# Output projection of all token tiles but the last, done inside the attention stage of a two-layer diffusion backbone

## The chip, the cores and the metric
One Trainium2 chip, one of its eight cores. The metric is the device time of one execution of the whole kernel in microseconds (us), as the median of several executions. Before the change three executions took 1636.07, 1642.16 and 1647.30 us, so the median is 1642.16 us.

## The reference
The kernel computes a two-layer backbone over 256 latent tokens and 256 context tokens of width 1024, all in fp32. Each layer is a mixer followed by a mixture of experts; the parts that matter here are these (layer 0 mixes with latent attention and a linear recurrence, layer 1 with windowed attention and a state-space model):

```python
# mixer, either layer: heads of attention beside a recurrence, then one output projection
y_l = jnp.concatenate([attn_l, other_l], axis=-1) @ w_out      # w_out: 1024 x 1024
# the layer adds it to the stream through a gate row, normalises, and routes to experts
x = x + gate * y
h = rmsnorm(x, norm2_g) * (1 + scale) + shift
x = x + gate2 * moe_ffn(h, router_w, router_b, w_gate, w_up, w_down)
# moe_ffn: 32 experts of 3 x 1024 x 512 weights, each token goes to its best two
```

Layer 0 does this for latent and context tokens, layer 1 for latent tokens alone.

## The kernel before
The tokens lie in tiles of 128: tiles 0 and 1 are latent, 2 and 3 context. Layer 0 works on four tiles, layer 1 on two. The kernel is a series of stages. Each stage is a block in which every engine has its own program in order, engines meet only by semaphores, and nothing of the next block starts before the block ends. For one layer the stages that matter are `attention_stage`, `output_front_stage`, `experts_stage` and a combine stage.

**Attention** (L856 to L1029). The work is a list of units, one head of one tile, tile by tile: 32 units in layer 0, 16 in layer 1, taken in pairs (16 and 8 pairs; four pairs finish a tile). In turn `j` of TensorE's loop (L934) it computes the scores of pair `j+1` (`score`), turns the probabilities of the two units of pair `j` through the identity (`turn`), and multiplies those of pair `j-1` with the values (`values`). ScalarE copies turned probabilities out and takes exponentials. VectorE finds the maxima, divides the probabilities by their sum (L1017, L1018), which is what `turn` waits for, and then copies the finished pair `j-1` out of bank 6 (`copy_out`, L1004). Units of the latent tiles see 4 blocks of keys, those of the context tiles 2. In layer 0 six products of the late modulation rows (`md`) are put after `values` of turns 3, 5, 7, 9, 11 and 13, in bank 7 (L943 to L949); VectorE takes each one out a turn later. SyncE loads their weights and `w_out` here (L882, L2255); in layer 1 it loads `w_out` and the first expert weights, a third of slot 2 and a spare one (L2293 to L2298).

**Output and router** (`output_front_stage`, L1103 to L1380). TensorE multiplies each tile's 1024 mixed features by `w_out` in half tiles of 512 columns (`project`, L1184), rotating over four banks. A half tile is 8 matmuls of 128x128 by 128x512; the profile shows an fp32 matmul as two instructions. VectorE multiplies the bank by the gate row and adds it to the token stream (`add`, L1257 and L1258), ScalarE squares the finished tile and takes the root (`root`, L1155), VectorE scales it (`scale`, L1261), and TensorE turns it (L1193). After the last tile the router's products follow, the choice of experts on VectorE, and the ranks. Before its first `add`, VectorE waits for the router's small tables (L1274).

**SyncE's order in that stage** (L1128 to L1146) is gate rows, modulation columns, router tables, then `first_weights`: rows of the norm, and in layer 0 the whole of expert 0 and the down matrix of expert 1. Slot 1 of the expert weights is where `w_out` lies, so its gate and up matrices wait for all projections (L1136); those of slot 2 wait for the last `add` (L1138), the rest for `h_ready` and `part_logits`. In layer 0 GpSimd writes 4 MB of zeros to spare blocks meanwhile.

**Experts** (`experts_stage`, L1428). There are three slots (`RING`), so three experts and a spare down matrix can be there before the stage begins. From then on SyncE loads the next expert into a slot when the gate and up product of its last block is done (L1462). An expert is 6 MB.

The lines that set the order around the change:

```python
            for j in range(pairs):                     # TensorE, attention, L934
                ...score of pair j+1; turn(2 * j); turn(2 * j + 1)
                if j:
                    values(j - 1)
                if j in ada_after: ...md.product(a, 7)
```

Of the kernel before, what the change touches and what calls it, by code (L numbers as in the profile page):

```python
# [20 lines left out]
ALU = mybir.AluOpType  # L21
# [3 lines left out]
P = 128  # L25
D = 1024
KC = D // P
SEQ = 256
NT = 4
# [826 lines left out]
def attention_stage(c, units, qt, kt, v_of, scale, dst_t, p, pt, width, sink=None, mask=None, sp_work=None, md=None):  # L856
# [11 lines left out]
    if md:  # L868
        ada_after = {3 + a * (pairs - 6) // (md.n - 1): a for a in range(md.n)}
        ada_in = [c.sem(f"ada_w_in{j}") for j in range(len(md.ring))]  # L870
        ada_product, ada_done, stored, preset, tables_in, columns = (
            c.sem(x) for x in ("ada_product", "ada_row_done", "mod_stored", "mod_tables_preset", "mod_tables_in", "cond_columns"))
    nm, rs, es = ([c.stat[:, a + s:a + s + 1] for s in range(4)] for a in (0, 4, 8))

# [3 lines left out]
    with nc.Block() as block:  # L878
        @block.sync
        def _(sp):  # L880
            if md:
                for a in range(len(md.ring)):  # L882
                    if a == 1:
                        sp.wait_ge(tables_in, 16 * md.n_loads)
                    md.load_weights(sp, a, ada_in[a])
            if sp_work:
                sp_work(sp)
            if md:
                R = len(md.ring)
                for a in range(R, md.n):  # L890
                    sp.wait_ge(ada_product, a - R + 1)
                    md.load_weights(sp, a, ada_in[a % R])
                sp.wait_ge(ada_done, md.n)
                md.store(sp, stored)
                sp.wait_ge(stored, 16 * md.Q * len(md.segments))
# [9 lines left out]
        def _(pe):  # L905
# [28 lines left out]
            for j in range(pairs):  # L934
                for u in (2 * j + 2, 2 * j + 3):
                    if u < n:
                        score(u)
                turn(2 * j)
                turn(2 * j + 1)
                if j:  # L940
                    values(j - 1)
                if j in ada_after:
                    a = ada_after[j]  # L943
                    if a == 0:
                        pe.wait_ge(columns, 1)
                    else:
                        pe.wait_ge(ada_done, a)
                    pe.wait_ge(ada_in[a % len(md.ring)], 16 * (a // len(md.ring) + 1))
                    md.product(a, 7).then_inc(ada_product, 1)  # L949
            values(pairs - 1)  # L950
# [26 lines left out]
        def _(dve):  # L977
# [32 lines left out]
            for u in range(n):  # L1010
                k0 = units[u][2]
                dve.wait_ge(exp_r, u + 1)
                den = rs[u % 4]
                if sink is not None:
                    dve.wait_ge(den_r, u + 1)
                    step(nc.vector.tensor_tensor(den, den, es[u % 4], ALU.add))
                step(nc.vector.reciprocal(den, den))  # L1017
                nc.vector.tensor_scalar(p[:, u % 4, k0 * P:T], p[:, u % 4, k0 * P:T], den, None, ALU.mult).then_inc(p_ready, 1)  # L1018
                if u + 2 < n:
                    maximum(u + 2)  # L1020
                j = u // 2
                if u % 2 and j:
                    copy_out(j - 1)
                    if j - 1 in ada_after:
                        if ada_after[j - 1] == 0:
                            dve.wait_ge(tables_in, 16 * md.n_loads)
                        dve.wait_ge(ada_product, ada_after[j - 1] + 1)
                        md.finish(ada_after[j - 1], 7, ada_done)
# [4 lines left out]
YB = 4  # L1033

# [68 lines left out]
def output_front_stage(c, m, tiles, wo, halves, gates_at, tmp_at, sp_work, pool_work=None, pool_done=None):  # L1103
# [5 lines left out]
    gate_in, product, taken = S("out_gate_in"), S("out_product"), S("out_added")  # L1109
# [9 lines left out]
    gates = [c.scr[:, gates_at + s * D:gates_at + (s + 1) * D] for s in streams]  # L1119
    tmp = c.scr[:, tmp_at:tmp_at + BANK]  # L1120
    units = [(t, q) for t in tiles for q in range(2)]
# [4 lines left out]
    with nc.Block() as block:  # L1126
        @block.sync
        def _(sp):  # L1128
            for s in streams:
                sp.dma_start(gates[s], mod_row(c, s, m.layer, 2)).then_inc(gate_in, 16)  # L1130
# [5 lines left out]
            sp.wait_ge(product, len(units))  # L1136
            load_gate_up(c, m, sp, 1, 1)
            sp.wait_ge(taken, len(units))  # L1138
# [15 lines left out]
        def _(act):  # L1154
            def root(t):  # L1155
                act.wait_ge(taken, 2 * t + 2)
# [26 lines left out]
        def _(pe):  # L1183
            def project(u):  # L1184
                t, q = units[u]
                if u >= 4:
                    pe.wait_ge(taken, u - 3)
                for k in range(KC):
                    src = halves[k // 4][:, k % 4, t * P:(t + 1) * P]
                    last = nc.tensor.matmul(c.ps[u % 4][:], src, wo[:, k, q * BANK:(q + 1) * BANK], start=k == 0, stop=k == KC - 1)  # L1190
                last.then_inc(product, 1)

# [11 lines left out]
            def part_product(s):  # L1204
# [5 lines left out]
                pe.wait_ge(taken, len(units) if s else 2 * nt - 3)  # L1210
# [7 lines left out]
            for t in tiles:  # L1218
                project(2 * t)
                project(2 * t + 1)  # L1220
                if t:
                    turn(t - 1)
# [3 lines left out]
            turn(nt - 1)  # L1226
# [23 lines left out]
        def _(dve):  # L1250
            step, go, wait, v = c.dve_chain.step, c.dve_chain.go, c.dve_chain.wait, nc.vector

            def add(u):
                t, q = units[u]
                dve.wait_ge(product, u + 1)
                cols = slice(q * BANK, (q + 1) * BANK)
                step(v.tensor_tensor(tmp, c.ps[u % 4][:], gates[t // LT][:, cols], ALU.mult))  # L1257
                step(v.tensor_tensor(c.x[:, t, cols], c.x[:, t, cols], tmp, ALU.add))  # L1258
                dve.sem_inc(taken, 1)
# [28 lines left out]
            dve.wait_ge(gate_in, 16 * len(streams))  # L1288
            for t in tiles:
                add(2 * t)  # L1290
                if t:
                    scale(t - 1)
                if t == NT - 1:
                    dve.wait_ge(m.rows_in, 16 * len(streams))
                    rows(0)
                    rows(1)
                add(2 * t + 1)
            scale(nt - 1)
# [927 lines left out]
def program(nc, ins, outs):  # L2226
    with ExitStack() as ctx:
# [29 lines left out]
        def clear_spare_blocks(pool):  # L2257
# [4 lines left out]
            for r in parts:  # L2262
# [3 lines left out]

        units = [(h, t, 0 if t < LT else LT) for t in everyone for h in range(NH)]
        attention_stage(c, units, m.qt, lambda h: m.kt[:, h, :], lambda h, k: m.v[:, k, h * VD:(h + 1) * VD],
                        QK ** -0.5, m.attn_t, m.p, m.pt, QK, sp_work=loads, md=last)
# [9 lines left out]
        output_front_stage(c, mo, everyone, m.wo, (m.attn_t, m.gr), 9216, 3072, first_weights, clear_spare_blocks, blocks_cleared)  # L2279
# [13 lines left out]
        def loads(sp):  # L2293
# [5 lines left out]

        units = [(h, t, 0) for t in range(LT) for h in range(NH)]  # L2300
        attention_stage(c, units, m.qt, lambda h: m.kt[:, h // (NH // KVH), :],
                        lambda h, k: m.kv[:, k, KVH * HD + h // (NH // KVH) * HD:KVH * HD + (h // (NH // KVH) + 1) * HD],
                        HD ** -0.5, m.attn_t, m.p, m.pt, HD, sink=m.sink, mask=lambda t: (1 - t, m.far[:, t, :]), sp_work=loads)
# [4 lines left out]
        output_front_stage(c, mo, range(LT), m.wo, (m.attn_t, m.y_t), 9216, 8192, first_weights)  # L2308
# [49 lines left out]
```

## Time and profile before

| | us |
|---|---|
| median of three executions | 1642.16 |
| lowest, highest | 1636.07, 1647.30 |
| the profiled execution | 1640.26 |
| its span on the core | 1638.4 |
| TensorE matmul busy | 1231.4 (75%) |
| TensorE weight load busy (beside matmul) | 716.8 (44%) |
| VectorE busy | 540.6 (33%) |
| ScalarE busy | 404.5 (25%) |
| bytes moved | 515.12 MB, mean 314 GB/s |

All durations in this document come from that one profiled execution, whose 1640.26 us are its span of 1638.4 us and 1.9 us around it. The busy shares are averages over stages with different limits; what bounds a stage is read from that stretch alone. PE is TensorE, PEld its weight load, DVE VectorE, ACT ScalarE, POOL GpSimd, SP SyncE (SPq its queue). "<-" in brackets names what ended the idle time ahead of an instruction.

### The profile page before, as it was taken

The page shows a single profiled execution, that of the slowest core. Times are in us where ns is not written, and L with a number is a line of the kernel's source. Part 1 is how long each engine was busy: PE and PEld are TensorE (multiplying, and loading weights), DVE is VectorE, ACT ScalarE, POOL GpSimd, SP SyncE. Part 2 cuts the span into 40 slices and gives each one's busy share as a digit, 9 for nine tenths or more (in the row PEclk, how much of TensorE's full clock was granted, in tenths as well). Part 3 has the DMA queues.
Part 4 walks back from the last instruction along what each step waited for, and adds up shares of the span by engine and source line. Part 5 has one row for each costly group of instructions (what it writes and reads, how often), then busy time and mean ns, then how long its engine had stood idle before and what let it go on. Part 6 is the DMA issues. An engine that isn't in the chain of part 4 may idle for free. (4 is left out here: it accounts for less than half of the span.)

```text
span 1638.4 us, 34883 instructions
## 1 busy us (share of the span) xinstructions
PE 1231.4 (75%) x14230; PEld 716.8 (44%) x14231; DVE 540.6 (33%) x1490; ACT 404.5 (25%) x927; POOL 39.3 (2%) x83
## 2 busy tenths in 40 slices
PE   4897887897799997777662898888579766655652
PEld 3354654543465554444331646544345433322321
DVE  1537564526322222111113456873511111101102
ACT  1253233412132222212202222641122221111110
POOL 0001101010000000000001000000000000000000
PEclk8899898998899998989886899979699887777776
DMA  8311896485899999999996410083799999999995
GB/s 312 121 67 39 305 379 248 171 318 247 342 416 429 429 428 430 428 429 429 429 428 251 170 52 0 1 359 105 332 419 428 429 429 429 429 428 428 429 428 208
DMA packets 84160, 515.12 MB, mean 314 GB/s; under 512 B 13917, under 2 KB 18242, under 8 KB 58746
## 3 DMA queue, kind: packets, MB, share of 16 engines
q1 hardware_dynamic: 74664, 489.60, 72.8%
q10 hardware_dynamic: 5730, 13.81, 2.2%
q0 software_dynamic: 3696, 10.73, 1.7%
q8 instruction: 50, 0.82, 0.2%
q14 instruction: 20, 0.16, 0.0%
HBM read 497.10 MB, written 17.01 MB: 314 GB/s over the span
## 5 line engine op out<-in xcount | busy, mean ns | idle before, releaser
L1509 PE MATMUL bank<-sb_ring,sb_scratch 128*32 128x256 f32 x3904 | 272.8, 441 | 150.4 <-DMA sb_ring<-in_moe_w_up 138.9
L1509 PEld LDWEIGHTS bank<-sb_ring,sb_scratch 128*32 128x32 f32 x3904 | 144.7, 127 | 276.1 <-issue 220.9
L1590 DVE TENSOR_TENSOR sb_scratch<-sb_scratch,bank 128x128 f32<-128x128 f32 x88 | 25.3, 288 | 700.3 <-ACT sb_scratch L1543 700.3
L1547 ACT ACTIVATE sb_scratch<-bank 32x256 f32<-32x256 f32 x352 | 131.8, 374 | 273.8 <-PE bank L1519 270.7
L1509 PE MATMUL bank<-sb_scratch 128*32 128x256 f32 x1728 | 118.7, 436 | 60.8 <-DMA sb_scratch<-in_moe_w_up 56.6
L1489 PE MATMUL bank<-sb_h,sb_scratch 128*32 128x256 f32 x2256 | 141.1, 384 | 6.1 <-DVE sb_scratch L1577 6.1
L1543 ACT ACTIVATE sb_scratch<-bank 128x128 f32<-128x128 f32 x88 | 24.4, 277 | 423.8 <-PE bank L1509 423.7
L1519 PE MATMUL bank<-sb_ring,sb_scratch 128*32 128x256 f32 x1856 | 111.5, 380 | 8.5 <-issue 8.2
L1509 PEld LDWEIGHTS bank<-sb_scratch 128*32 128x32 f32 x1728 | 62.2, 125 | 116.0 <-issue 91.8
L1489 PEld LDWEIGHTS bank<-sb_h,sb_scratch 128*32 128x32 f32 x2256 | 74.8, 111 | 54.8 <-DVE sb_scratch L1577 6.6
L1519 PEld LDWEIGHTS bank<-sb_ring,sb_scratch 128*32 128x32 f32 x1856 | 62.7, 110 | 51.2 <-issue 19.8
L1190 PE MATMUL bank<-sb_ring,sb_scratch 128*128 128x512 f32 x160 | 69.9, 593 | 0.6 <-PEq L878 0.6
L1921 PE MATMUL bank<-sb_ht,sb_ring 128*128 128x512 f32 (+1 forms) x192 | 64.9, 496 | 0.0
L551 PE MATMUL bank<-sb_ht,sb_ring 128*128 128x512 f32 x128 | 58.3, 618 | 6.8 <-PEq L253 6.8
L1519 PE MATMUL bank<-sb_scratch 128*32 128x256 f32 x864 | 51.9, 380 | 4.5 <-issue 4.1
L1582 DVE STREAM_TRANSPOSE sb_scratch<-bank 128x256 f32<-128x256 f32 x90 | 38.9, 432 | 37.4 <-PE bank L1489 37.4
L194 PE MATMUL bank<-sb_ring 128*32 128x128 f32 x1344 | 44.4, 291 | 8.6 <-DMA sb_ring<-in_ada_w 8.6
L1921 PEld LDWEIGHTS bank<-sb_ht,sb_ring 128*128 128x128 f32 x192 | 36.6, 193 | 25.8 <-issue 23.6
L1190 PEld LDWEIGHTS bank<-sb_ring,sb_scratch 128*128 128x128 f32 x160 | 30.2, 190 | 37.7 <-issue 37.7
L194 PEld LDWEIGHTS bank<-sb_ring 128*32 128x32 f32 x1344 | 39.1, 117 | 15.8 <-DMA sb_ring<-in_ada_w 10.3
L551 PEld LDWEIGHTS bank<-sb_ht,sb_ring 128*128 128x128 f32 x128 | 25.3, 199 | 39.0 <-issue 39.0
L1519 PEld LDWEIGHTS bank<-sb_scratch 128*32 128x32 f32 x864 | 29.4, 110 | 24.2 <-issue 9.7
(362 smaller groups left out, 1380.6 us busy)
## 6 DMA issues: line engine op xcount, KB each, us to landing
sb_ring<-in_moe_w_gate SPq DMA_DIRECT2D x44, 2048.0 KB, 27.4
sb_ring<-in_moe_w_up SPq DMA_DIRECT2D x44, 2048.0 KB, 32.0
sb_ring<-in_moe_w_down SPq DMA_DIRECT2D x41, 2048.0 KB, 34.7
sb_ring<-in_ada_w SPq DMA_DIRECT2D x21, 2048.0 KB, 15.1
sb_scratch<-in_moe_w_gate SPq DMA_DIRECT2D x20, 2048.0 KB, 30.7
sb_scratch<-in_moe_w_up SPq DMA_DIRECT2D x20, 2048.0 KB, 33.8
sb_scratch<-in_moe_w_down SPq DMA_DIRECT2D x20, 2048.0 KB, 36.1
sorted_out<-sb_scratch ACTq DMA_DIRECT2D x88, 128.0 KB, 6.1
```

The lines of the kernel that those rows point to most:

```text
L194: last = self.c.nc.tensor.matmul(self.c.ps[bank][32 * q:32 * q + 32, 0:P], self.condk[:, k, :], w[:, k, q * P:(q + 1) * P], start=k == 0, ...
L551: last = nc.tensor.matmul(c.ps[u % NB][:, 0:rhs.shape[1]], lhs, rhs, start=k == 0, stop=k == KC - 1)
L1190: last = nc.tensor.matmul(c.ps[u % 4][:], src, wo[:, k, q * BANK:(q + 1) * BANK], start=k == 0, stop=k == KC - 1)
L1489: last = nc.tensor.matmul(c.ps[0][MB * q:MB * q + MB, 0:DQ], m.pick[:, t, :], c.h[:, t, q * DQ:(q + 1) * DQ], start=t == 0, stop=t == nt - 1)
L1509: last = nc.tensor.matmul(c.bank(1, 2, FQ)[MB * q:MB * q + MB, :, :], m.xt[:, k, :], m.gu[j][:, :, k, q * FQ:(q + 1) * FQ], start=k == 0, ...
L1519: last = nc.tensor.matmul(c.ps[3][MB * q:MB * q + MB, 0:DQ], m.hmt[:, k, :], down[k][:, q * DQ:(q + 1) * DQ], start=k == 0, stop=k == DE / ...
L1543: nc.scalar.activation(m.sg, c.ps[1][:, 0:FQ], ACT.Silu).then_inc(silu_r, 1)
L1547: last = nc.scalar.activation(m.yb[j][:, q * DQ:(q + 1) * DQ], c.ps[3][MB * q:MB * q + MB, 0:DQ], ACT.Copy)
L1582: v.transpose(m.xt, c.bank(0, MB, KC).rearrange("p j k -> p k j")).then_inc(xt_ready, 1)
L1590: v.tensor_tensor(m.hm, m.sg, c.ps[1][:, FQ:2 * FQ], ALU.mult).then_inc(hm_ready, 1)
L1921: last = nc.tensor.matmul(c.ps[bank_of(u)][:, 0:rhs.shape[1]], lhs, rhs, start=k == 0, stop=k == KC - 1)
```

## The change
The products of `w_out` for all tiles but the last one move from `output_front_stage` into `attention_stage`: six half tiles in layer 0, two in layer 1. A new class `Output` holds them. Half tile `u` is done in turn `out_after`: 6, 7, 10, 11, 14 and 15 in layer 0, and 6 and 7 in layer 1. It stands between the scores and the turns of that turn of the loop, always in bank 7, and VectorE takes it out and adds it after `copy_out` in the same turn. The modulation products move to the same place in the loop and to turns 3, 4, 5, 8, 9 and 12. The gate rows are loaded first in the attention's stage. The front stage keeps the two half tiles of the last tile, in banks 1 and 2, with the turns of earlier tiles before and between them.

```diff
-        ada_after = {3 + a * (pairs - 6) // (md.n - 1): a for a in range(md.n)}
+        ada_after = dict(zip((3, 4, 5, 8, 9, 12), range(md.n)))
...
+    by_tile = NH // 2
+    out_after = {by_tile * (u // 2 + 1) + 2 + u % 2: u for u in range(out.ahead)}
...
         def _(sp):
+            out.load_gates(sp, out_gate_in)
...
                 for u in (2 * j + 2, 2 * j + 3):
                     if u < n:
                         score(u)
-                turn(2 * j)
-                turn(2 * j + 1)
-                if j:
-                    values(j - 1)
+                if j in out_after:
+                    u = out_after[j]
+                    pe.wait_ge(out.wo_in, 16)
+                    pe.wait_ge(out_r, by_tile * (u // 2 + 1))
+                    if u:
+                        pe.wait_ge(out_added, u)
+                    if md:
+                        pe.wait_ge(ada_done, len([b for b in ada_after if b < j]))
+                    out.product(u, 7).then_inc(out_product, 1)
                 if j in ada_after:
                     a = ada_after[j]
+                    if out_after and j > min(out_after):
+                        pe.wait_ge(out_added, len([b for b in out_after if b < j]))
...
                     md.product(a, 7).then_inc(ada_product, 1)
+                turn(2 * j)
+                turn(2 * j + 1)
+                if j:
+                    values(j - 1)
...
                     copy_out(j - 1)
-                    if j - 1 in ada_after:
...
+                    if j in ada_after:
...
+                    if j in out_after:
+                        if out_after[j] == 0:
+                            dve.wait_ge(out_gate_in, 16 * len(out.streams))
+                        dve.wait_ge(out_product, out_after[j] + 1)
+                        if out_after[j]:
+                            dve.wait_ge(out_added, out_after[j])
+                        out.add(out_after[j], 7, out.tmps[0]).then_inc(out_added, 1)
...
+class Output:
...
+    def product(self, u, bank):
+        t, q = self.units[u]
+        for k in range(KC):
+            src = self.halves[k // 4][:, k % 4, t * P:(t + 1) * P]
+            last = self.c.nc.tensor.matmul(self.c.ps[bank][:], src, self.wo[:, k, q * BANK:(q + 1) * BANK], start=k == 0, stop=k == KC - 1)
+        return last
+
+    def add(self, u, bank, tmp):
+        (t, q), c, v = self.units[u], self.c, self.c.nc.vector
+        cols = slice(q * BANK, (q + 1) * BANK)
+        c.dve_chain.step(v.tensor_tensor(tmp, c.ps[bank][:], self.gates[t // LT][:, cols], ALU.mult))
+        return v.tensor_tensor(c.x[:, t, cols], c.x[:, t, cols], tmp, ALU.add)
...
             sp_work(sp)
-            sp.wait_ge(product, len(units))
+            sp.wait_ge(product, 2)
             load_gate_up(c, m, sp, 1, 1)
-            sp.wait_ge(taken, len(units))
+            sp.wait_ge(taken, 2)
...
-            for t in tiles:
-                project(2 * t)
-                project(2 * t + 1)
-                if t:
-                    turn(t - 1)
+            out.product(out.ahead, 1).then_inc(product, 1)
+            for t in range(min(LT, last_tile)):
+                turn(t)
+            out.product(out.ahead + 1, 2).then_inc(product, 1)
+            for t in range(LT, last_tile):
+                turn(t)
...
+            for t in range(min(LT, last_tile)):
+                scale(t)
+            add(0)
+            for t in range(LT, last_tile):
+                scale(t)
...
+            dve.wait_ge(taken, 1)
+            add(1)
+            scale(last_tile)
```

## Rows read from the trace of the kernel before

**Rows 1.** The profile's GB/s in 40 slices of 41 us each.
```profile
GB/s 312 121 67 39 305 379 248 171 318 247 342 416 429 429 428 430 428 429 429 429 428 251 170 52 0 1 359 105 332 419 428 429 429 429 429 428 428 429 428 208
```

**Rows 2.** Windows: stretch, length, PE busy, granted clock, DMA share, GB/s.
```profile
255.90:335.00 79.10, 65.80 (x736) 0.96 0.59 215
335.00:376.50 41.50, 41.47 (x103) 1.00 0.98 390
376.50:392.50 16.00, 16.00 (x49) 1.00 0.01 2
392.50:423.50 31.00, 12.29 (x88) 0.59 0.98 406
423.50:430.00 6.50, 5.86 (x96) 0.86 0.02 5
1130.00:1145.00 15.00, 15.00 (x40) 1.00 0.01 4
1170.00:1178.00 8.00, 6.87 (x80) 0.61 0.12 50
```

**Rows 3.** Timeline of SP: start, duration, weight loads into the slots.
```profile
392.00 0.33 SPq L1390 DMA_DIRECT2D sb_ring<-in_moe_w_gate  x1
...
429.57 0.33 SPq L1390 DMA_DIRECT2D sb_ring<-in_moe_w_gate  x1
...
1178.41 0.33 SPq L1390 DMA_DIRECT2D sb_ring<-in_moe_w_gate  x1
```

**Rows 4.** Timeline of PE in layer 0's front stage, [idle before].
```profile
363.46 13.90 PE L1190 MATMUL bank<-sb_ring,sb_scratch 128*128 128x512 f32 x32
377.19 1.04 PE L1200 MATMUL bank<-sb_ident,sb_h 128*128 128x128 f32 x8
...
421.50 1.08 PE L1489 MATMUL bank<-sb_h,sb_scratch 128*32 128x256 f32 x8 [3.34 <-DVE sb_scratch L1577]
```

**Rows 5.** Waits in layer 0's attention: total us, times, longest.
```profile
PE bank L918 <- DVE sb_scratch L1018: 11.9, 18, 1.1
```

**Rows 6.** Timeline of one turn of two key blocks, PE and DVE.
```profile
321.26 0.44 PE L918 MATMUL bank<-sb_ident,sb_scratch 128*128 128x128 f32 x2 [0.75 <-DVE sb_scratch L1018]
...
322.22 1.13 PE L910 MATMUL bank<-sb_scratch,sb_ht 96*128 96x256 f32 x4
322.34 0.29 DVE L1004 COPY sb_scratch<-bank 128x128 f32<-128x128 f32 x1 [0.61 <-PE bank L928]
```

**Rows 7.** Timeline of DVE in layer 0's front stage.
```profile
349.63 0.09 DVE L1275 MEMSET sb_scratch<- 128x32 f32 x1 [14.19 <-DMA sb_scratch<-in_before]
...
351.26 0.69 DVE L1257 TENSOR_TENSOR sb_scratch<-bank,sb_scratch 128x512 f32<-128x512 f32 x1
351.99 0.69 DVE L1258 TENSOR_TENSOR sb_x<-sb_x,sb_scratch 128x512 f32<-128x512 f32 x1
...
393.08 0.69 DVE L1258 TENSOR_TENSOR sb_x<-sb_x,sb_scratch 128x512 f32<-128x512 f32 x1
```

**Rows 8.** The load of layer 0's w_out: issue; and us to landing.
```profile
266.37 1.33 SPq L2255 DMA_DIRECT2D sb_ring<-in_ab_w_out  x1
...
sb_ring<-in_ab_w_out SPq DMA_DIRECT2D x1, 4096.0 KB, 23.5
```

**Rows 9.** Timeline of PE, layer 1: attention's end and front stage.
```profile
1109.43 0.66 PE L918 MATMUL bank<-sb_ident,sb_ring 128*128 128x128 f32 x4 [1.20 <-DVE sb_ring L1018]
...
1112.29 1.44 PE L918 MATMUL bank<-sb_ident,sb_ring 128*128 128x128 f32 x8 [1.18 <-DVE sb_ring L1018]
...
1116.99 3.67 PE L1190 MATMUL bank<-sb_ring,sb_ht 128*128 128x512 f32 x8 [0.65 <-PEq L878]
...
1144.53 1.05 PE L1200 MATMUL bank<-sb_ident,sb_h 128*128 128x128 f32 x8
1148.85 1.95 PE L1200 MATMUL bank<-sb_ident,sb_h 128*128 128x128 f32 x8 [3.27 <-DVE sb_h L1264]
```

**Rows 10.** Timeline of DVE in layer 1's front stage.
```profile
1122.88 0.09 DVE L1275 MEMSET sb_scratch<- 128x32 f32 x1 [5.49 <-DMA sb_scratch<-in_before]
```

## What the change will do to the time

> **What bounds the kernel now.** I read the data rate by slice first. It stands at 428 to 430 GB/s for most of two long stretches, slices 12 to 21 and 29 to 39 [rows 1]: those are the two experts stages, and there the transfer of weights is the bound, not an engine. What moves the end of such a stretch is when its stream of weights begins and how often it stands still before it runs full. Second, the windows of layer 0's front stage show where it stands still: 16.0 us with a DMA share of 0.01 (376.5 to 392.5), and 6.5 us more at 0.02 (423.5 to 430) [rows 2]. The queue's timeline says why [rows 3]: slot 1 holds w_out, so its load goes out only at 392.00, when all projections are done; and the first refill goes out at 429.57, when expert 0's first product is done. In layer 1 the same two holes are 15 us (1130 to 1145) and some 7 us (1170 to 1178) [rows 2], and the first refill goes out at 1178.41 [rows 3]. Third, TensorE: from 335.0 to 392.5 it is busy without a break [rows 2], and in the attention before it 65.8 of 79.1 us. So TensorE's work sets the time through both stages, and the weights wait for it, but only in part: of the 95 us from 335.0 to the first refill's data at 430, 72.5 are taken by transfers.
>
> **What a moved half tile costs.** Two half tiles take 377.19 - 363.46 = 13.73 us [rows 4], so one is 6.87 us at a granted clock of 1.00. Six move in layer 0: 41.2 us of TensorE leave the front stage and enter the attention, where the clock is 0.96 on average [rows 2], so they cost the same there.
>
> **What the attention hides of it.** TensorE waits 11.9 us in all for the divided probabilities, in 18 waits [rows 5]. It is mostly the second turn of a pair, 0.75 us in the turn shown [rows 6]. Twelve of the sixteen turns get a product ahead of `turn` (six half tiles, six modulation products), and behind it the probabilities are ready. I take 12/16 of 11.9 = 8.9 us as saved. Ends: nothing saved, and all of TensorE's idle time, 79.1 - 65.8 = 13.3 us.
>
> **What is late next.** All new products use bank 7, and each waits until VectorE has taken the one before out. VectorE does that after `copy_out`, which starts 322.34 - 322.22 = 0.12 us after the next scores start [rows 6]. Then come 0.29 for the copy and 1.42 for the two halves of an `add` (351.26 to 351.99 + 0.69 [rows 7]), with the hand-overs some 1.9 us after the scores start. Scores of two key blocks fill about 1.0 us of that [rows 6]. So TensorE waits some 1.0 us in turns 7, 8, 11 and 12, and in turn 15, where there are no scores, 1.9: together 5.9. In turns 10 and 14 a modulation product was in between and the adds are long done. Queued behind VectorE's adds are the divisions of the next pair, which the next product covers; where nothing covers them, the stage ends 0.3 us later. Ends for this term: 0 and 11.4 (six times 1.9).
>
> The rotation of banks bears on the same step. The Trainium skill, page "Perfetto Trace Analysis", section "Matmuls", says that independent groups of matmuls should go round several PSUM banks, so that taking one out overlaps the next group's products. The front stage before does so, the new code does not; by that rule rotating would save the 5.9 us here and 1.9 in layer 1, and the change gives them away. The rows above give the price without it.
>
> Costed at nothing: the gate rows (1 MB) at the head of the attention's queue, hidden by the holes in its transfers (share 0.59 over the stage [rows 2]), at most 2.7 us if they push a weight that a product waits for; w_out, needed in turn 6 at about 293, lands at 266.37 + 23.5 = 289.9 [rows 8], so a wait is unlikely and would be 1 or 2 us; the modulation products in new turns, same work.
>
> So layer 0's attention grows by 41.2 - 8.9 + 5.9 + 0.3 = **38.5 us**.
>
> **What the front stage of layer 0 gives back.** Two clocks run in it. TensorE's: the tables that VectorE waits for land 14.6 us after the stage's start (349.63 - 335.0 [rows 7]), and its setup ends 1.6 us later; now that hides nothing any more. With two scales and two turns, about 2 us each as an estimate, the second half tile starts near 20 and ends near 27, the last add near 28. From the last add (393.08 + 0.69) to the first gather is 27.7 us [rows 4, 7], to the first refill 8.1 more [rows 3]. So the experts begin at 56 after the start instead of 86.5, and the first refill goes out at 64.
> The weights' clock: none of their loads starts before the stage does, for slot 0 is the modulation's ring until then and slot 1 is w_out. Their volume takes 41.5 + 31.0 us in the two full windows [rows 2], less 2% idle 71.1; the gate rows, 2.7 us at 390 GB/s, are gone from it; with the start-up it is **69 us**. The slots' waits (projections at 27, last add at 28) now come before the queue runs dry. 69 is later than 64, so the stream of weights never stops and it, not TensorE, sets when the refills' data begin: 69 after the start, against 95. That is 26 us back, not 41. Layer 0: 38.5 - 26 = **+12.5 us**. The full stream behind it [rows 1] carries this to the layer's end.
>
> **Layer 1.** Two half tiles are 13.7 us. Waits of 1.20 and 1.18 us [rows 9] go, 1.9 comes in the last turn, and 0.3 at the end: +13.5. In the front stage the four half tiles end 1144.53 - 1116.99 = 27.5 us after its start [rows 9]. Now the tables (1122.88 - 1116.99 = 5.9 [rows 10]), setup 1.6, a scale of about 1 and a turn of 1.05, less 0.4 for the gate row's issue, put the second half tile at 9.1, its end at 16.0: -11.5. Everything behind, refill and stream, hangs on that end as before, since the weights have a hole of 7 us there. Layer 1: **+2.0 us**.
>
> **Sum.** The profiled execution took 1640.26, so 1640.3 + 12.5 + 2.0 = 1654.8, say **1655 us**. The median of the runs, 1642.16, is 1.9 above the profiled time, so this is 0.8% over it. About 1% (16.4 us, so 1658.6) is what a measurement of this kernel can tell from no change.
>
> **Rivals.** (a) *Not slower: the attention swallows more.* If the chain of ScalarE and VectorE never holds TensorE and bank 7 is always free in time, all 13.3 us of idle time in layer 0's attention go and no wait comes: 27.9 - 26 = +1.9. In layer 1 likewise the 2.4 us of waits go and none comes: 11.3 - 11.5 = -0.2. That gives 1642.0. For it: the new products are dense and the waits small. Against it: the waits for bank 7 follow from the code and the rows. It decides from a growth of layer 0's attention under about 30 us. Chance 0.19.
> (b) *Slower by over 1%: TensorE's clock falls in the front stage.* After 3.27 us of idle the same eight turns take 1.95 us instead of 1.05 [rows 9]: 1.2 instead of 2.4 GHz. Now TensorE idles between the two half tiles of the front stage, by my numbers 1.3 us in layer 1 and some 9 us in layer 0. If the second half tile and the turn run at the lower level, layer 1 pays 6.9 + 0.9 = 7.8 us; layer 0's refills go out at 72.5 instead of 64, 3.4 past the stream. That gives 1655 + 11.2 = 1666, or 1663 for layer 1 alone. It decides from whether the wait in layer 1 stays near 1.3 us. Chance 0.18.
> On this the Trainium skill, page "TensorE: Matmul & The Clock Gate", section "What's actually happening", says that half rate is the default and only activity releases it, which would halve the rate at least in layer 0.
> (c) *Faster by over 1%.* It needs a stream that is not the bound. But even TensorE's own clock in layer 0 gives 38.5 - (86.5 - 56) = +8. I find no mechanism: 0.05.
>
> **How the numbers follow.** My forecast has 0.58; its own range is 1650 to 1660, and 0.08 of its chance lies over 1658.6. Faster 0.05; within 1%: 0.50 + 0.19 = 0.69; slower 0.08 + 0.18 = 0.26. The range 1643 to 1665 holds the forecast, most of (b) and the upper part of (a), whose ends come from the bounds of the hidden share and of bank 7's waits.
>
> **What would show it.** In the profile of the changed kernel: layer 0's attention about 117 us long; waits of about 1 us ahead of products in turns 7, 8, 11 and 12; no slice of idle transfers between its end and the end of the experts; the first refill issued before the queue is empty; layer 1's first refill about 2 us later against layer 1's attention start. The prediction is wrong if the attention grows by under 30 us or if weights still stand still for more than a few us in layer 0's front stage.

## The result and the profile after

The changed kernel takes 1650.95 us against 1637.95 us for the kernel before (medians of 20 runs each on one chip); the ratio is 1.0058 with a 95% interval of 1.0044 to 1.0072. That is 9.5 us, between 7.2 and 11.8. One execution of the changed kernel took 1918.62 us at a mean granted clock of 0.634 and is left out of the ratio. The medians by themselves differ by more, 13.0 us: the other 19 fall in two groups, six from 1641.44 to 1645.69 and thirteen from 1647.82 to 1653.91, and the median lies in the upper one. The profiled execution has a span of 1647.2 us against 1638.4 before, so +8.8. It is slower, by less than the 1% that counted as telling, and by less than the +14.5 of my sum.

I read the page's data rates first, the row that answers to [rows 1]:

```profile
GB/s 310 133 53 52 322 348 297 140 21 417 424 431 425 430 428 429 429 430 429 428 429 232 166 51 1 2 368 84 311 418 427 429 428 431 429 428 428 431 428 211
```

Counted from 0, slice 8 (329 to 371 us) has fallen from 318 to 21 GB/s: layer 0's attention now lasts to the end of it, with its own loads done. From slice 9 on the rate is near its full height, where before there were 247 and 342 in slices 9 and 10. The stream of weights starts later and then doesn't stop up to the end of this layer's experts. The windows put numbers to it; these answer to [rows 2] (stretch, length, PE busy, granted clock, DMA share, GB/s):

```profile
254.10:366.30 112.20, 102.44 (x831) 0.99 0.44 158
366.30:373.00 6.70, 6.70 (x16) 1.00 0.65 228
373.00:404.00 31.00, 19.28 (x89) 0.71 1.02 422
404.00:421.70 17.70, 4.01 (x16) 0.50 1.00 428
421.70:430.00 8.30, 7.61 (x100) 0.69 1.00 422
430.00:440.00 10.00, 9.63 (x184) 1.00 1.01 424
```

The first window begins 2 us into the attention's stage; from its first scores (252.10) the stage lasts 114.2 us, where the prediction had about 117. The two holes of before (16.0 us at 0.01 and 6.5 us at 0.02) are gone: from 373 on the share is 1.00 to 1.02. TensorE is the one that is idle now, busy 19.3 of 31.0 us and then 4.0 of 17.7. The slots' loads on SP's queue, and the loads behind them, in the profile after (start, duration):

```profile
392.19 0.33 SPq L1427 DMA_DIRECT2D sb_ring<-in_moe_w_gate  x1
395.09 0.33 SPq L1427 DMA_DIRECT2D sb_scratch<-in_moe_w_gate  x1
...
430.21 0.33 SPq L1427 DMA_DIRECT2D sb_ring<-in_moe_w_gate  x1
...
1187.38 0.33 SPq L1427 DMA_DIRECT2D sb_ring<-in_moe_w_gate  x1
```

Slot 1's load goes out at 392.19, 25.9 us after the stage's start (57 before), and layer 0's first refill at 430.21, 63.9 us after it (94.5 before). In absolute time 430.21 is no earlier than the 429.57 of [rows 3]: all that the front stage saved had been spent in the attention. And the data of this refill begin later than its issue, for the queue is still full. When they begin can be had from the bytes that all queues move from the stage's start to the refill's data, first before, then after:

```profile
335.00:430.00 95.00, 75.62 (x328) 0.86 0.75 303
366.26:434.80 68.54, 42.04 (x300) 0.70 0.98 404
```

Before, 95.0 us at 303 GB/s are 28.8 MB, of which the gate rows (1.05 MB) have moved to the attention. The 27.7 MB that are left have moved in the changed kernel at 434.8, so the refill's data begin 68.5 us after the stage's start.

How the front stage's saving was spent in the attention is in TensorE's timeline:

```profile
288.62 7.13 PE L1077 MATMUL bank<-sb_ring,sb_scratch 128*128 128x512 f32 x16
295.59 1.04 PE L922 MATMUL bank<-sb_ident,sb_scratch 128*128 128x128 f32 x8
...
299.57 7.10 PE L1077 MATMUL bank<-sb_ring,sb_scratch 128*128 128x512 f32 x16 [0.86 <-DVE sb_x L1084]
...
310.29 1.96 PE L194 MATMUL bank<-sb_ring 128*32 128x128 f32 x64 [0.66 <-DVE sb_x L1084]
...
355.99 7.11 PE L1077 MATMUL bank<-sb_ring,sb_scratch 128*128 128x512 f32 x16 [1.91 <-DVE sb_x L1084]
...
366.30 7.11 PE L1077 MATMUL bank<-sb_ring,sb_scratch 128*128 128x512 f32 x16 [1.04 <-PEq L881]
380.90 3.67 PE L1239 MATMUL bank<-sb_ident,sb_h 128*128 128x128 f32 x16 [7.50 <-DVE sb_h L1296]
384.38 7.79 PE L1077 MATMUL bank<-sb_ring,sb_scratch 128*128 128x512 f32 x16
...
421.75 3.64 PE L1526 MATMUL bank<-sb_h,sb_scratch 128*32 128x256 f32 x32 [3.34 <-DVE sb_scratch L1614]
```

A half tile takes 295.59 - 288.62 = 6.97 us. The turns behind it follow with no wait. The waits of products for bank 7 are there, 0.86 and 0.66 in turns 7 and 8, 0.86 and 0.65 in turns 11 and 12, and 1.91 in turn 15. The sums of the waits, to be compared with [rows 5] (total us, times, longest):

```profile
PE bank L1077 <- DVE sb_x L1084: 3.6, 3, 1.9
PE bank L922 <- DVE sb_scratch L1033: 3.2, 5, 1.0
...
PE bank L194 <- DVE sb_x L1084: 1.3, 2, 0.7
```

The waits for divided probabilities fall from 11.9 to 3.2 us, and 4.9 us of waits for bank 7 come. Layer 0's front stage still opens with the tables, as in [rows 7], now 378.26 - 366.3 = 12.0 us after its start:

```profile
378.26 0.09 DVE L1307 MEMSET sb_scratch<- 128x32 f32 x1 [11.55 <-DMA sb_scratch<-in_before]
```

Layer 1, TensorE, which answers to [rows 9]:

```profile
1087.10 3.78 PE L914 MATMUL bank<-sb_scratch 64*128 64x512 f32 x4
...
1126.07 5.37 PE L1077 MATMUL bank<-sb_ring,sb_ht 128*128 128x512 f32 x8 [1.81 <-DVE sb_x L1084]
...
1139.00 3.67 PE L1077 MATMUL bank<-sb_ring,sb_ht 128*128 128x512 f32 x8 [0.65 <-PEq L881]
...
1146.24 1.16 PE L1239 MATMUL bank<-sb_ident,sb_h 128*128 128x128 f32 x8
```

In layer 1 a half tile shows as two rows of eight instructions. The last one in the attention waits 1.81 us for bank 7. The front stage runs half tile, turn, half tile without a gap. The first row is a matter of its own: here the scores of a pair take 3.78 us where the same pairs took 1.98 before. TensorE was at 0.50 of its clock (1.2 GHz) from 1085 to 1100, two pairs longer than in the profile of before. What that is worth is told below, since most of it has to be kept out of the change's account.

### The profile page after: what moved, and what is told of

The parts are those of the page before. It is cut to its first block and busy times, and to the rows that moved or that the text cites. A ratio compares the mean times of both kernels' runs of the same rounds, so it can differ in the third digit from the quotient of the medians.

```text
span 1647.2 us, 34894 instructions
## 1 busy us (share of the span) xinstructions
PE 1236.1 (75%) x14230; PEld 716.5 (43%) x14231; DVE 539.0 (33%) x1490; ACT 403.2 (24%) x927; POOL 39.5 (2%) x83
## 5 line engine op out<-in xcount | busy, mean ns | idle before, releaser
L1546 PEld LDWEIGHTS bank<-sb_ring,sb_scratch 128*32 128x32 f32 x3904 | 141.6, 126 | 277.3 <-issue 219.8
L1546 PEld LDWEIGHTS bank<-sb_scratch 128*32 128x32 f32 x1728 | 62.3, 126 | 120.1 <-issue 95.5
L1556 PEld LDWEIGHTS bank<-sb_ring,sb_scratch 128*32 128x32 f32 x1856 | 62.5, 110 | 51.5 <-issue 19.0
```

Source lines behind the costliest of these rows:

```text
L1546: last = nc.tensor.matmul(c.bank(1, 2, FQ)[MB * q:MB * q + MB, :, :], m.xt[:, k, :], m.gu[j][:, :, k, q * FQ:(q + 1) * FQ], start=k == 0, ...
L1556: last = nc.tensor.matmul(c.ps[3][MB * q:MB * q + MB, 0:DQ], m.hmt[:, k, :], down[k][:, q * DQ:(q + 1) * DQ], start=k == 0, stop=k == DE / ...
```

## The experiments

All ratios are to the kernel before, from runs on the same chip, with their 95% interval. Where two of these ratios are compared, the difference has both intervals in it, some 4 us either way. "First turn" is the start of the attention's first turn, "front" the start of layer 0's front stage.

**1. Layer 0 alone, layer 1 alone.** The changed functions serve one layer and the old ones the other, in outline:

```
# layer 0 moved            # layer 1 moved
attention_stage(... out)   attention_stage_before(...)      # layer 0
output_front_stage(...)    output_front_stage_before(...)
attention_stage_before     attention_stage(... out)         # layer 1
output_front_stage_before  output_front_stage(...)
```

> The changed attention and front stage in layer 0 alone, layer 1 as in the kernel before. My theory: layer 0's attention grows by some 35 us and the weights' stream, which cannot start before the front stage, gives back only some 26, so nearly all of the loss is here: 7 to 9 us over the kernel before (ratio 1.004 to 1.006), first refill of the slots about 64 us after the front stage's start with transfers never idle before it. Rival (the loss is layer 1's, where the changed trace shows 6 us more between the attention's start and the first refill): 3 to 4 us here.

> The changed stages in layer 1 alone, layer 0 as before. My theory: +13.5 in the attention, -11.5 to -13 in the front stage, so 1 to 2 us over the kernel before (ratio 1.0005 to 1.0015). Rival (layer 1 carries the loss): 6 us.

Layer 0 alone: 1645.34 us, 1.0031 (1.0007 to 1.0054), so +5.1 us. Layer 1 alone: 1638.74 us, 0.9999 (0.9975 to 1.0024). A loss shows only with layer 0 changed. In layer 1 none can be told from zero, within 4 us either way, which rules out the 6 us of the rival. In the profile of layer 0 alone, first turn to front takes 366.57 - 258.29 = 108.3 us, as in the whole change (366.30 - 257.92 = 108.4), against 335.0 - 262.45 = 72.5 before. In layer 1's, attention start to first refill takes 1173.99 - 1061.94 = 112.05 us, against 111.9 before. The two ratios together give +4.9 where the whole measured +9.5; with some 4 us of uncertainty on each of the two, that doesn't contradict it, and doesn't settle it.

**2. The modulation's order alone.** The kernel before, with only its six modulation products moved ahead of the turns:

```
-        ada_after = {3 + a * (pairs - 6) // (md.n - 1): a for a in range(md.n)}
+        ada_after = dict(zip((3, 4, 5, 8, 9, 12), range(md.n)))
...
+                if j in ada_after:        # the product, now ahead of the turns
                 turn(2 * j)
                 turn(2 * j + 1)
```

> The kernel before, with only the six modulation products moved ahead of the turns of their pair and to turns 3, 4, 5, 8, 9 and 12; the output projection stays in the front stage. My theory: each hides the wait ahead of one or two turns (0.5 to 1.1 us), so layer 0's attention is 3 to 4.5 us shorter and the kernel too, since TensorE sets the time up to the first refill: ratio 0.997 to 0.998. If placing products ahead of the turns hides nothing, no change.

1635.92 us, 0.9972 (0.9956 to 0.9988). First turn to front is 327.41 - 259.45 = 68.0 us, 4.6 less than before, and the waits say where it comes from:

```profile
PE bank L918 <- DVE sb_scratch L1018: 7.3, 10, 0.9
```

11.9 - 7.3 = 4.6. So six products hide what my term gave them (half of 8.9), and this part of the change is a gain by itself, and the loss comes with the moved projections.

**3. What the start of the stream holds back.** In the changed kernel nothing of the experts is loaded before the stage boundary, though slot 0 is free after the last modulation product. Three things can be moved ahead of the boundary: expert 0, the router's tables of both layers (which TensorE's path waits for), and the zeros for the spare blocks.

```
# expert 0 in the attention, behind the last modulation product
                 md.store(sp, stored)
+                if sp_late:
+                    sp_late(sp)            # load_expert(c, mo, sp, 0, 0)
# router tables in the attention, behind w_out
             sp.dma_start(m.wo, ...).then_inc(wo_in, 16)
+            load_router(c, mo, sp)
# zeros for the spare blocks in the attention's POOL block
+                    pool.wait_ge(ada_product, 4)
+                    pool_late(pool)        # clear_spare_blocks
```

First expert 0 alone:

> The changed kernel, but layer 0's expert 0 (6 MB) is loaded in the attention's stage, after the last modulation product has freed its slot. My theory, the stream of weights sets the first refill's data at about 69 us after the front stage's start and TensorE would allow 64: about 4.5 us faster than the changed kernel, so 4 to 5 us over the kernel before (ratio 1.002 to 1.004), and transfers idle for some 8 us ahead of the first refill. Rival (TensorE's own path sets it): as the changed kernel, 9 us over the kernel before.

1645.23 us, 1.0019 (0.9996 to 1.0041). The time from front to layer 1's attention falls from 703.3 to 699.7 us. The windows around the refill show why it is no more (the third column is POOL's here). The changed kernel:

```profile
424.00:430.00 6.00, 0.00 (x0) 0.76 0.98 412
```

and the one with expert 0 early:

```profile
424.00:430.00 6.00, 0.00 (x0) 0.50 0.35 143
430.00:436.00 6.00, 0.00 (x0) 1.00 0.36 106
```

The stream now runs dry ahead of the refill, which comes at 432.99 - 369.55 = 63.4 us after front. The bound has passed from the stream to TensorE's path, which had reached the refill 4.6 us before the stream did (63.9 against 68.5).

Then the tables alone:

> The changed kernel with the router's tables loaded in the attention's stage of both layers, so that the front stage's second half tile need not wait for them. My theory (stream of weights sets layer 0's first refill): TensorE's path in layer 0's front stage is some 8 to 10 us shorter, but the kernel at most 1 us faster than the changed one, 8.5 to 9.5 over the kernel before. Rival (TensorE's path): 8 to 10 us faster than the changed kernel, level with the kernel before.

1646.86 us, 1.0044 (1.0025 to 1.0062). The refill comes 62.3 us after front instead of 63.9, though TensorE no longer waits for the tables there. What took the gain is first in SP's queue:

```profile
422.46 0.33 SPq L1426 DMA_DIRECT2D sb_scratch<-in_moe_w_gate  x1
...
434.43 0.33 SPq L1426 DMA_DIRECT2D sb_ring<-in_moe_w_gate  x1
```

and then in TensorE's timeline:

```profile
426.38 3.60 PE L1525 MATMUL bank<-sb_h,sb_scratch 128*32 128x256 f32 x32 [10.53 <-DVE sb_scratch L1613]
```

Slot 2's loads wait in the code for the zeros of the spare blocks, which POOL's queue writes. They now go out 50.3 us after front (28.8 in the changed kernel), so the zeros come late, though they were issued as soon after the start as before. That SP's weights, which now enter their queue sooner (3.0 us after the start instead of 7.2), hold them up is an inference. The stage can't end before SP has issued these loads, and so the gather, the experts' first product, has waited 10.53 us. TensorE's shorter path is lost in a third wait, and from front to layer 1's attention this profile has 705.7 us, no less than the 703.3 of the changed kernel.

Then both together, and all three:

> The changed kernel with both: expert 0 of layer 0 and the router's tables loaded in the attention's stage. My theory: TensorE would allow the first refill some 54 us after the front stage's start and the stream 54, so 14 to 15 us faster than the changed kernel, 4 to 6 us faster than the kernel before (ratio 0.996 to 0.9975). If the two gains were separate and not two bounds on the same point, it would be the sum of what each gives alone.

> As the one with both, and GpSimd's 4 MB of zeros are written in the attention's stage too, after the fourth modulation product. That takes 10 us off the transfers of layer 0's front stage, but my theory has TensorE's path as the bound by now: 0 to 2 us faster than with both, 5 to 7 us faster than the kernel before (ratio 0.9955 to 0.997). If transfers are still the bound, up to 10 us faster than with both.

Both: 1633.61 us, 0.9967 (0.9951 to 0.9983); the refill 54.1 us after front, front to layer 1's attention 690.8 us. All three: 1632.64 us, 0.9957 (0.9942 to 0.9972). SP's refill with both:

```profile
423.09 0.33 SPq L1428 DMA_DIRECT2D sb_ring<-in_moe_w_gate  x1
```

and the window ahead of the refill with all three (POOL's column third):

```profile
418.00:424.00 6.00, 0.00 (x0) 0.99 0.19 38
```

By the ratios the tables alone gave 2.3 us, which the intervals don't tell from nothing, expert 0 alone 6.4 (3.6 in its profile), and both together 15. There are two clocks in this stage, the stream's and that of TensorE's path, and shortening one leaves the other. For expert 0 the windows show just that; for the tables alone the late zeros came in between, so there it isn't shown separately. With both, slot 2's loads go out at 404, 34.7 us after front. With all three the stream stands nearly still (0.19) ahead of the refill at 422.20, so TensorE's path is the bound, and what the early zeros add, about 1 us, can't be told from nothing.

**4. The same early loads without the change.** Is it the change that makes them pay?

```
# kernel before, expert 0 behind the last modulation product
+                    sp_late(sp)            # load_expert(c, mo, sp, 0, 0)
# and, in the second kernel, load_router behind w_out as above
```

> Control: the kernel before with the same early load of expert 0. There transfers already stand still for 16 and 7 us before the first refill, and TensorE sets it: no change, within 1.5 us of the kernel before. If the volume of transfers counted by itself, it would be some 14 us faster.

> The kernel before with expert 0 of layer 0 and the router's tables of both layers loaded in the attention's stage, the tables ahead of the expert. The same load of expert 0 alone cost 11 us. If that was because the small tables stood behind 6 MB in SyncE's queue, this one is level with the kernel before, within 1.5 us. If an early load costs for another reason (bandwidth taken from somebody, the longer stage), it is again 11 us slower. It is not faster in either case, since TensorE sets the first refill.

Expert 0 alone: 1653.01 us, 1.0068 (1.0047 to 1.0089), where I had expected no change. SP, VectorE and TensorE in it:

```profile
339.28 4.91 SPq L1425 DMA_DIRECT2D sb_scratch<-in_router_b  x1
344.25 6.01 SPq L1426 DMA_DIRECT2D sb_scratch<-in_count  x1
...
365.82 0.09 DVE L1277 MEMSET sb_scratch<- 128x32 f32 x1 [30.37 <-DMA sb_scratch<-in_before]
...
374.41 1.97 PE L1202 MATMUL bank<-sb_ident,sb_h 128*128 128x128 f32 x8 [11.66 <-DVE sb_h L1266]
...
405.42 0.33 SPq L1392 DMA_DIRECT2D sb_ring<-in_moe_w_gate  x1
```

The tables stand behind 6 MB in one queue. VectorE gets them at 365.82 instead of 349.63 [rows 7], TensorE idles 11.66 us, and slot 1's load slips from 392.00 to 405.42. With the tables loaded ahead: 1644.24 us, 1.0018 (0.9999 to 1.0037), some 3 us over no change, where I had expected at most 1.5. Most of the 11 us is gone. SP and TensorE in this kernel show what is left:

```profile
332.86 6.40 SPq L1419 DMA_DIRECT2D sb_scratch<-mod  x2
...
362.95 1.97 PE L1201 MATMUL bank<-sb_ident,sb_h 128*128 128x128 f32 x8 [4.54 <-DVE sb_h L1265]
...
431.49 0.33 SPq L1391 DMA_DIRECT2D sb_ring<-in_moe_w_gate  x1
```

TensorE still idles 4.54 us. The tables are early, but the small loads of the modulation still go out behind the 6 MB (6.40 us to issue two), and VectorE's first add waits for one of them:

```profile
353.88 0.69 DVE L1258 TENSOR_TENSOR sb_scratch<-bank,sb_scratch 128x512 f32<-128x512 f32 x1 [20.86 <-DMA sb_scratch<-mod]
```

It comes 23.2 us after the stage's start. So these early loads are worth nothing to the kernel before, where TensorE's projections set when the slots come free. After the change both are worth 15 us.

**5. Bank 7 taken out first.** On VectorE all that is taken out of bank 7 (the adds and the modulation's products) comes ahead of the copy of the pair's output, in the same bank and with nothing else changed:

```
                 if u % 2 and j:
-                    copy_out(j - 1)
                     if j in ada_after:
...
                         out.add(out_after[j], 7, out.tmps[0]).then_inc(out_added, 1)
+                    copy_out(j - 1)
```

> The changed kernel with only that order on VectorE. My theory: the attention's stages end some 4.9 and 1.8 us sooner, and since both the stream of weights and TensorE's path start at the stage's end, the kernel is 5 to 7 us faster than the changed one, 2 to 4 us over the kernel before. Rival (the waits for bank 7 are covered by something else that then ends the wait): as the changed kernel, 9 us over.

> As the one with expert 0, tables and zeros early, and in the attention's loop VectorE takes bank 7 out before it copies out the pair, so the next product in bank 7 finds it free. The waits ahead of such products are 4.9 us in layer 0 and 1.8 in layer 1 in the changed kernel's trace. My theory: TensorE's path sets the first refill in both layers here, so they come off in full: 6 to 7 us faster than with all early, 13 us faster than the kernel before (ratio about 0.992). If VectorE's new order delays the turns' probabilities instead, no gain.

On the changed kernel: 1640.20 us, 1.0001 (0.9979 to 1.0022). TensorE's waits in layer 0's attention:

```profile
PE bank L922 <- DVE sb_scratch L1033: 2.5, 4, 0.8
...
PE bank L1077 <- DVE sb_scratch L1019: 0.7, 1, 0.7
```

and its products there and, last, in layer 1:

```profile
298.87 7.03 PE L1077 MATMUL bank<-sb_ring,sb_scratch 128*128 128x512 f32 x16
...
361.46 7.11 PE L1077 MATMUL bank<-sb_ring,sb_scratch 128*128 128x512 f32 x16 [0.65 <-PEq L881]
...
1113.93 3.70 PE L1077 MATMUL bank<-sb_ring,sb_ht 128*128 128x512 f32 x8
```

The waits for the adds are gone but for 0.7 us, now behind the copy. First turn to front is 361.46 - 258.95 = 102.5 us, 5.9 less than in the changed kernel: 4.2 of the waits for bank 7, 0.7 behind the probabilities and 0.4 at the boundary make 5.3 of it. In layer 1 the product at 1113.93 has no wait ahead of it, but little of that arrives: from the attention's start to the first refill it takes 111.8 us, against the 112.05 of layer 1 alone. In the front stage TensorE now idles 1.68 us ahead of its first turn (0.40 there), because VectorE is still held by the router's tables.

With all loads early on top: 1623.77 us against 1639.39, **0.9885 (0.9863 to 0.9907)**, where I expected about 0.992; the medians alone, with six executions, give 0.9905. This is the fastest version, and it beats both kernels. Its refill, in SP's timeline:

```profile
418.88 0.33 SPq L1431 DMA_DIRECT2D sb_ring<-in_moe_w_gate  x1
```

and the windows of its front stage ahead of it (PE's column third):

```profile
364.60:400.00 35.40, 24.18 (x108) 0.83 0.81 327
400.00:410.00 10.00, 2.94 (x14) 0.50 0.98 419
410.00:418.00 8.00, 6.84 (x88) 0.66 0.32 134
```

The refill is 54.3 us after front (364.58), and the first turn to it takes 418.88 - 262.02 = 156.9 us, against 167.1 before and 422.20 - 257.69 = 164.5 with the early loads alone. In layer 1, where the tables are early too, the removed wait now arrives: 109.1 us from the attention's start to the first refill, against 111.7 with the early loads alone. The share of 0.32 ahead of it says what would come next: TensorE's path through the router, at the low clock, not the stream.

## Why the prediction was right, and where its size was off

**Layer 0's attention: +38.5 forecast, +35.8 measured** (108.3 - 72.5, from the first turn). The six half tiles, each from its start to that of the turns behind it, cost 41.5 (41.2 forecast). The waits for bank 7 cost 4.9 (5.9), each in the turn in which the prediction put it. The probabilities' waits gave back 11.9 - 3.2 = 8.7 (8.9). The part that I had not seen is the turns themselves: with all probabilities ready, two turns of four key blocks run together in 1.04 us, where before they took 0.60 and 0.66 on either side of the wait, and two of two blocks in 0.60 instead of 0.38 and 0.44. That is some 0.2 a time, so an estimated 12 x 0.2 = 2.4 more are saved. The boundary took 0.4 more. That is 41.5 + 4.9 - 8.7 - 2.4 + 0.4 = 35.7, 0.1 under the measured growth.

**Front stage: -26 forecast, -28.3 measured** (731.6 to 703.3 us from front to layer 1's attention). Both clocks were as forecast: TensorE's path to the refill 63.9 us (64), the gather at 55.4 (56), and a stream without a hole from 373 on, with the refill's data at 68.5 (69). That the first of these fits so closely is partly luck: the tables came 12.0 us after the start instead of 14.6, and the low clock that the forecast had left to rival (b) took some 2 us of that back. What the forecast left out is that the stream, where it has stood still, is not at its full rate at once:

```profile
430.00:435.00 5.00, 4.64 (x88) 1.00 0.92 331
430.00:435.00 5.00, 4.63 (x90) 1.00 1.03 428
```

Before, where the refill finds empty queues, the first 5 us run at 331 GB/s (first row), and after at 428 (second row): 1.1 us more are saved. With 95.0 - 68.5 = 26.5 that is 27.6 of the 28.3; the rest is open. Layer 0 in all: +7.5 instead of +12.5, and layer 0 alone has +5.1 (1.1 to 8.9) by its ratio.

**Layer 1: +2.0 forecast, +0.2 measured in the profile** at like clock: 112.05 us from attention start to refill with layer 1 alone against 111.9 before. The front stage gave back 13.0 us (61.4 to 48.4) instead of 11.5, since the second half tile follows the turn with no idle time between them. The changed kernel's own profile has 1187.38 - 1069.50 = 117.9, 6.0 more. Two pairs at 7.68 us instead of 5.38 are 4.6 of this, and the row at 5.37 instead of 3.67 is 1.7: both are the clock's level (0.50 from 1085 to 1100, 0.67 from 1126.07 to 1131.28). The long phase isn't the change's, for the kernels with the old attention in layer 1 showed it too, 115.0 us with layer 0 alone and with the modulation's order alone, and others with the new one didn't, 111.7 with both loads early. But the new attention pays more in it: 117.9 here and with expert 0 early, 2.9 over those 115.0. The slow row behind the wait of 1.81 us stands only in these two profiles; where the phase was short, the same wait was followed by a row of 3.67 us. So in the long phase the change costs layer 1 some 3 us, and in the short one nothing to speak of. What picks the one or the other is open.

**Which step failed.** None of the mechanism; three terms were mis-sized, each by about 2 to 3 us and all on the same side: the attention by 2.7 (the turns that run together), what the front stage gives back by 2.3 (0.5 in when the refill's data begin, 1.1 in the restart of the idle stream, the rest open), layer 1 by 1.8 in the short phase. Together some 7 of the 14.5 us. So that the profiled pair shows +8.8 is not the sum coming true: it is +7.5 from layer 0, 6.0 from layer 1 in its long phase, and 4.5 less ahead of the first turn (257.92 instead of 262.45), 3.8 of it before the attention's stage, where nothing was changed.

**The rivals.** (a) Not slower: refuted; the attention grew by 35.8, over the 30 from which it decides, and the waits came. With the adds first no loss can be measured any more: 1.0001 (0.9979 to 1.0022). (b) The clock falls in the front stage. In layer 0 it did: 16 turns took 3.67 us after 7.50 idle, at a granted clock of 0.50, and the half tile 7.79 at 0.90. It cost nothing, because the refill's data hung on the stream and not on TensorE. In layer 1 it didn't: the idle time of 1.3 us didn't come, and the turn took 1.16. With the adds first such a gap did come, 1.68 us, and the turn took 1.16 all the same. The Trainium skill, page "TensorE: Matmul & The Clock Gate", section "What's actually happening", says that the clock is throttled by default and released by activity; layer 0's rows agree. (c) Faster: not by this change; it took other loads with it.

**The banks.** The Trainium skill's page "Perfetto Trace Analysis", section "Matmuls", asks for independent groups to go round several banks. The rows agree that one bank costs: 4.9 us here and 1.8 in layer 1. But the experiment removed the waits in the same bank, by VectorE's order alone, and gained 9.3 us by the ratios (1.0058 to 1.0001). The waits and what hangs on them are 5.9 of it in layer 0; in layer 1, at like clock, only 0.3 of the 1.8 reaches the refill. The rest lies within what the intervals and the clock's phase leave open. A version that goes round several banks was not run.

## What to carry to other kernels

Work that moves to an earlier stage is worth what it hides there, here 11.1 of 41.5 us, and what the later stage can use of the time. Where a stream of weights bounds the later stage and starts at the boundary, pushing the boundary back costs time that a shorter path in the later stage can't buy back: move the start of the stream along, with the small loads ahead of the large ones, and then shorten the engines' path, both, since either alone leaves the other clock. And when a product shares its bank, look at what the engine that empties it does first: its order may be all that costs.

## What the runs showed that I had not expected

A full queue of large loads holds up what is small. Behind 6 MB, the issue of a small load on SP took 4.91, 6.01 and 6.40 us instead of the 0.60, 2.45 and 2.20 us of the same loads before, and tables that were there 14.6 us after the stage's start came at 30.8. It may reach over to another queue, though no run tests that alone: the zeros that POOL's queue writes let SP go on 28.8 us after the start in the changed kernel and 50.3 us when SP's loads began earlier. And the same kernel's untouched stages aren't always alike: in the profiles layer 0's attention starts at 251.6 to 255.9 us though nothing ahead of it was changed, and layer 1's opens with TensorE at 1.2 GHz for two pairs longer in some than in others. Differences of 3 to 6 us between single profiles mean little until those two are taken out.
